# mLSTM tiles: waits by scan direction, the next tile's mask products and scores moved between this tile's products, and output tiles gated earlier

## The reference, cut to what matters

```python
dmat = jnp.where(mask, b[..., :, None] - b[..., None, :] + ic[..., None, :], -jnp.inf)
s = jnp.einsum('bhtd,bhsd->bhts', qc, kc) * jnp.exp(dmat - m_t[..., None])
num = w_inter[..., None] * jnp.einsum('bhtd,bhde->bhte', qc, cm) + jnp.einsum('bhts,bhse->bhte', s, vc)
den = w_inter * jnp.einsum('bhtd,bhd->bht', qc, nv) + s.sum(axis=-1)
h = num / jnp.maximum(jnp.abs(den), jnp.exp(-m_t))[..., None]
...
h = h_f + flip(h_b)
...
ha = rms_norm(ha.astype(xm.dtype), P['mlstm_norm_w'][j].reshape(A_HEADS, A_V_DIM)).reshape(bsz, n_tok, A_HEADS * A_V_DIM)
ha = ha * jax.nn.sigmoid(oa)
```

## Time and profile before

| | |
|---|---|
| median of 3 runs | 1601.32 us (1595.04 to 1603.25) |
| the profiled execution | 1601.95 us, span 1600.1 us, granted clock 0.918 |
| TensorE busy | 1356.6 us, 85% of the span |
| VectorE, ScalarE, GpSimd busy | 1002.8, 802.8, 428.6 us |

### The profile page before, as it was taken

How to read it: one execution, slowest core, us unless ns; L and a number is a source line. 1 busy time by engine, 2 the same in 40 slices (tenths; PEclk the granted TensorE clock), 3 DMA queues, 4 the chain that set the end, 5 groups by cost and what they waited for, 6 DMA issues and landing times. The chain is left out here.

```text
span 1600.1 us, 17702 instructions
## 1 busy us (share of the span) xinstructions
PE 1356.6 (85%) x6661; PEld 944.4 (59%) x6661; DVE 1002.8 (63%) x1331; ACT 802.8 (50%) x1135; POOL 428.6 (27%) x257
## 2 busy tenths in 40 slices
PE   3389998768779299999998999988779299999995
PEld 0366566744468166666666878654458266666663
DVE  0624623366564688888876625935554688888875
ACT  0421312354342277777775348554332277777772
POOL 0200203034400204433441021534400205433440
PEclk7699999689899599999998999999899599999997
DMA  9378860050051799999984012040051799999954
GB/s 358 145 285 340 310 227 16 1 197 1 1 212 66 279 341 367 385 378 379 379 307 118 1 57 57 5 197 1 1 203 74 272 344 366 384 381 383 380 183 163
DMA packets 64300, 341.73 MB, mean 214 GB/s; under 512 B 16796, under 2 KB 21512, under 8 KB 45784
## 3 DMA queue, kind: packets, MB, share of 16 engines
q1 hardware_dynamic: 58168, 319.96, 52.4%
q0 software_dynamic: 6048, 20.65, 5.5%
HBM read 316.67 MB, written 23.91 MB: 213 GB/s over the span
## 5 line engine op out<-in xcount | busy, mean ns | idle before, releaser
L1791 DVE TENSOR_TENSOR wlow<-wraw,proj_rounded 128x2048 fp32r<-128x2048 f32 x96 | 216.9, 2287 | 5.2 <-ACT proj_rounded L1733 5.2
L1641 POOL TENSOR_TENSOR modrow<-modrow,proj 80x1024 f32<-80x1024 f32 x30 | 133.2, 4439 | 309.2 <-ACT modrow L1759 309.2
L1670 PE MATMUL psum<-wlow,proj_rounded 128*80 128x512 f32 x512 | 202.4, 395 | 0.0
L1733 ACT ACTIVATE proj_rounded<-wraw 128x2048 fp32r<-128x2048 f32 x96 | 180.0, 1909 | 9.2 <-PEq L1322 9.2
L1669 PE MATMUL psum<-proj_rounded 128*80 128x512 f32 x376 | 151.3, 402 | 2.1 <-DVE proj_rounded L1796 2.1
L1671 PE MATMUL psum<-proj_rounded 128*80 128x512 f32 x376 | 148.6, 395 | 0.0
L1255 POOL TENSOR_SCALAR ring<-ring,small 128x640 f32<-128x640 f32 x64 | 100.0, 1566 | 167.4 <-DVE small L1202 166.6
L1228 ACT ACTIVATE ring<-psum,small 128x640 f32<-128x640 f32 (+1 forms) x80 | 56.7, 709 | 103.3 <-DVE small L1196 102.8
L1193 DVE TENSOR_REDUCE small<-psum 128x1 f32<-128x640 f32 (+1 forms) x80 | 57.2, 715 | 72.2 <-PE psum L1167 72.1
L1670 PE MATMUL psum<-wlow,small_rounded 128*80 128x512 f32 x256 | 100.8, 394 | 0.0
L1791 DVE TENSOR_TENSOR wlow<-wraw,xr_rounded 128x2048 fp32r<-128x2048 f32 x32 | 73.3, 2291 | 43.6 <-ACT xr_rounded L1733 43.6
(11 more groups left out here) (461 smaller groups left out, 3256.7 us busy)
## 6 DMA issues: line engine op xcount, KB each, us to landing
wraw<-in_exp_w_gate_dram SPq DMA_DIRECT2D x32, 2048.0 KB, 13.8
wraw<-in_exp_w_up_dram SPq DMA_DIRECT2D x32, 2048.0 KB, 12.6
wraw<-in_exp_w_down_dram SPq DMA_DIRECT2D x32, 2048.0 KB, 13.7
ring<-in_ada_w_dram SPq DMA_DIRECT2D x29, 1024.0 KB, 6.8
hold<-in_ada_w_dram SPq DMA_DIRECT2D x14, 1024.0 KB, 6.7
ring<-in_ev_w_in_dram SPq DMA_DIRECT2D x4, 2048.0 KB, 11.8
xr<-x_rows SPq DMA_DIRECT2D x15, 512.0 KB, 8.2
proj<-mod_rows SPq DMA_DIRECT2D x12, 512.0 KB, 5.5
```

The source lines that it names most:

```text
L1641: pool.tensor_tensor(ye[0:CAP, :], ye[0:CAP, :], g2[0:CAP, :], ALU.mult).then_inc(s["ye"], 1)
L1670: pe.matmul(dst, xs[:, 0, k, :], wl, start=False, stop=False)
L1733: act.activation(high_of(m, h), raw_of(m, h), ACT.Copy).then_inc(s["high"], 1)
L1791: dve.tensor_tensor(low_of(m, h), raw_of(m, h), high_of(m, h), ALU.subtract).then_inc(s["low"], 1)
```

## The change

- TensorE: mask products and scores of tile 0 come first. Then, within tile i, `bounds(i + 1, 0)` stands ahead of direction 0's products, and `bounds(i + 1, 1)` and `scores(i + 1)` stand between direction 0's and direction 1's. Direction 0's products wait for `fwd` only, direction 1's for `both`.
- ScalarE: `exponent(i + 1, 0)`, `forward(i)`, `exponent(i + 1, 1)`, `squares(i)`. `forward` waits for direction 0's divisors. Before the last `forward` it takes the square root for the first four tiles.
- VectorE: divisors by direction (`divisors(i, d)`), the rest of `normalise` as `backward(i)`, the next tile's weights between them. In the last tile the reciprocals of four tiles and the gating of the first one stand between the two directions' divisors, three more gatings after `backward`.
- `HA` lies in the columns of queries and keys (from `C_QA`); sums of squares and gatings go by the order of work.

```diff
--- before.py
+++ after.py
@@ -812,7 +812,7 @@
         def mlstm():
             s = {n: sem("ml_" + n) for n in ("kw", "upd", "carry", "qw", "qt", "qc", "ow",
                                              "mask", "E", "st", "W", "inter", "out", "own", "dn", "fwd", "both", "sq", "ssq", "root",
-                                             "ready", "turned", "copied", "h")}
+                                             "last_root", "ready", "turned", "copied", "h")}
             s2 = Carve(ringf)
             E = s2(2, 2, 4, P)
             CS = s2(2, ST - 1, 2, AV + 1)
@@ -823,7 +823,7 @@
             w = num_w
             dn = small[:, 0:8]
             ssq, rs = small[:, 32:52], small[:, 64:84]
-            HA = proj[:, :, C_VA:C_VA + AH * AV]
+            HA = proj[:, :, C_QA:C_QA + AH * AV]
             OA = proj[:, :, C_OA:C_OA + AH * AV]
 
             def turn_of(d, i):
@@ -914,30 +914,36 @@
                         mm.then_inc(s["out"], 1)
 
                     def turn(n):
+                        t = order[n]
                         pe.wait_ge(s["ready"], n + 1)
                         if n >= 4:
                             pe.wait_ge(s["copied"], n - 3)
                         for k in range(4):
-                            mm = pe.transpose(bank(n % 4)[:, k * P:(k + 1) * P], HA[:, n, k * P:(k + 1) * P], ident[:, :])
+                            mm = pe.transpose(bank(n % 4)[:, k * P:(k + 1) * P], HA[:, t, k * P:(k + 1) * P], ident[:, :])
                         mm.then_inc(s["turned"], 1)
 
                     for u in range(len(sums)):
                         add_sum(u)
                         turn_query(u)
                     pe.wait_ge(s["qc"], len(steps))
+                    bounds(0, 0)
+                    bounds(0, 1)
+                    scores(0)
                     for i, t in enumerate(order):
-                        bounds(i, 0)
-                        bounds(i, 1)
-                        scores(i)
+                        if i + 1 < TILES:
+                            bounds(i + 1, 0)
                         if i == 0:
                             pe.wait_ge(s["carry"], len(sums))
                         else:
                             pe.wait_ge(s["fwd"], i)
+                            from_state(i, 0)
+                        from_tile(i, 0)
+                        if i + 1 < TILES:
+                            bounds(i + 1, 1)
+                            scores(i + 1)
+                        if i:
                             pe.wait_ge(s["both"], i)
-                        for d in range(2):
-                            if t != PT:
-                                from_state(i, d)
-                        from_tile(i, 0)
+                            from_state(i, 1)
                         from_tile(i, 1)
                     for n in range(TILES):
                         turn(n)
@@ -955,7 +961,7 @@
                         ex.then_inc(s["E"], 1)
 
                     def forward(i):
-                        act.wait_ge(s["dn"], i + 1)
+                        act.wait_ge(s["dn"], 2 * i + 1)
                         for n in range(4):
                             r, j = n // 2, n % 2
                             h = 2 * j + r
@@ -972,20 +978,23 @@
                         t = turn_of(d, i)
                         act.wait_ge(s["qt"], n + 1)
                         act.activation(mq1[:, d, :, t * P:(t + 1) * P], bank(2 + n % 2, 256).rearrange("p (j c) -> p j c", j=2), ACT.Copy).then_inc(s["qc"], 1)
+                    exponent(0, 0)
+                    exponent(0, 1)
                     for i in range(TILES):
-                        exponent(i, 0)
-                        if i:
-                            forward(i - 1)
-                        exponent(i, 1)
-                        if i:
-                            squares(i - 1)
-                    forward(TILES - 1)
-                    squares(TILES - 1)
+                        if i + 1 < TILES:
+                            exponent(i + 1, 0)
+                        if i == TILES - 1:
+                            act.wait_ge(s["ssq"], i)
+                            act.activation(rs[:, 0:4 * i], ssq[:, 0:4 * i], ACT.Sqrt, scale=1.0 / AV, bias=EPS).then_inc(s["root"], 1)
+                        forward(i)
+                        if i + 1 < TILES:
+                            exponent(i + 1, 1)
+                        squares(i)
                     act.wait_ge(s["ssq"], TILES)
-                    act.activation(rs, ssq, ACT.Sqrt, scale=1.0 / AV, bias=EPS).then_inc(s["root"], 1)
-                    for n in range(TILES):
+                    act.activation(rs[:, 4 * TILES - 4:4 * TILES], ssq[:, 4 * TILES - 4:4 * TILES], ACT.Sqrt, scale=1.0 / AV, bias=EPS).then_inc(s["last_root"], 1)
+                    for n, t in enumerate(order):
                         act.wait_ge(s["turned"], n + 1)
-                        act.activation(xT[:, 4:8, n * P:(n + 1) * P], bank(n % 4).rearrange("p (k c) -> p k c", k=4), ACT.Copy).then_inc(s["copied"], 1)
+                        act.activation(xT[:, 4:8, t * P:(t + 1) * P], bank(n % 4).rearrange("p (k c) -> p k c", k=4), ACT.Copy).then_inc(s["copied"], 1)
 
                 @block.vector
                 def _(dve):
@@ -1020,20 +1029,22 @@
                         e4 = E[:, i % 2, d].rearrange("p (r j) n -> p r (j n)", r=2)
                         dve.tensor_tensor(e4, e4, psum[:, 0:2, 0:2 * P], ALU.mult).then_inc(s["W"], 1)
 
-                    def normalise(i):
+                    def divisors(i, d):
                         t = order[i]
-                        dve.wait_ge(s["out"], 2 * i + 2)
-                        if i:
+                        dve.wait_ge(s["out"], 2 * i + d + 1)
+                        if i and d == 0:
                             dve.wait_ge(s["fwd"], i)
-                        d8 = psum[:, 4:8, 0:258].rearrange("p b (j e) -> p b j e", e=129)[:, :, :, AV]
-                        d4 = d8.rearrange("p (d r) j -> p d r j", d=2)
-                        dn4 = dn.rearrange("p (d r j) -> p d r j", d=2, r=2)
-                        for d in range(2):
-                            neg = dve.scalar_tensor_tensor(out=dn4[:, d], in0=d4[:, d], scalar=-1.0, in1=col(2, d, t, 0, AH).rearrange("p (j r) -> p r j", r=2),
-                                                           op0=ALU.mult, op1=ALU.max)
-                        own.link(neg)
-                        own.link(dve.tensor_tensor(dn.rearrange("p (b j) -> p b j", j=2), dn.rearrange("p (b j) -> p b j", j=2), d8, ALU.max))
-                        dve.reciprocal(dn, dn).then_inc(s["dn"], 1)
+                        d4 = psum[:, 4 + 2 * d:6 + 2 * d, 0:258].rearrange("p r (j e) -> p r j e", e=129)[:, :, :, AV]
+                        own4 = dn[:, 4 * d:4 * d + 4]
+                        dn4 = own4.rearrange("p (r j) -> p r j", r=2)
+                        own.link(dve.scalar_tensor_tensor(out=dn4, in0=d4, scalar=-1.0, in1=col(2, d, t, 0, AH).rearrange("p (j r) -> p r j", r=2),
+                                                          op0=ALU.mult, op1=ALU.max))
+                        own.link(dve.tensor_tensor(dn4, dn4, d4, ALU.max))
+                        dve.reciprocal(own4, own4).then_inc(s["dn"], 1)
+
+                    def backward(i):
+                        t = order[i]
+                        dve.wait_ge(s["dn"], 2 * i + 2)
                         dve.wait_ge(s["fwd"], i + 1)
                         for n in range(4):
                             r, j = n // 2, n % 2
@@ -1044,9 +1055,8 @@
                         ins.then_inc(s["both"], 1)
 
                     def reduce(i):
-                        t = order[i]
                         dve.wait_ge(s["sq"], i + 1)
-                        dve.tensor_reduce(ssq[:, 4 * t:4 * t + 4], sq.rearrange("p (h d) -> p h d", d=AV), AX.X, ALU.add).then_inc(s["ssq"], 1)
+                        dve.tensor_reduce(ssq[:, 4 * i:4 * i + 4], sq.rearrange("p (h d) -> p h d", d=AV), AX.X, ALU.add).then_inc(s["ssq"], 1)
 
                     for u in range(4):
                         weigh_keys(u)
@@ -1054,22 +1064,37 @@
                         next_state(u)
                         if u + 4 < len(sums):
                             weigh_keys(u + 4)
-                    for i in range(TILES):
-                        weights(i, 0)
-                        weights(i, 1)
-                        if i:
-                            reduce(i - 1)
-                        normalise(i)
-                    reduce(TILES - 1)
-                    dve.wait_ge(s["root"], 1)
-                    own.link(dve.reciprocal(rs, rs))
-                    for t in range(TILES):
-                        dve.wait_ge(s["ow"], t + 1)
+                    def gated(n):
+                        t = order[n]
                         for h in range(AH):
                             sl = slice(h * AV, (h + 1) * AV)
```

(26 more changed lines are left out.)

## The result

The kernel after ran in 1576.80 us (median of 4 runs, 1575.80 to 1579.38), against 1600.41 us before (4 runs, 1595.04 to 1603.25): 0.9859 of the time, with a 95% interval of 0.9829 to 0.9888. Forecast were 1579.5, with 1572 to 1591. Two later series with the same kernel gave ratios of 0.9882 (0.9852 to 0.9912) and 0.9872 (0.9847 to 0.9898).

A forecast was written before the change was run, and what follows sets the result against it. No engine is full; a chain through several engines sets a 10.17 us period. The stage's last copy moves from 332.6 to 309.3, 23.3 us, less 1.3 for hand-overs: 22 us, 1601.32 to 1579.5, range 1572 to 1591.

The forecast's parts named there:

- The chain: Tile loop: waits through ScalarE, VectorE and TensorE set a period of 10.17 us, to become 4.76 with TensorE never waiting over 0.1.
- the allowance: 1.3 us taken off the 23.3 us gain for hand-overs that fit less closely, 0.3 in each of four periods.
- Prices at full clock: TensorE's work per tile, priced mostly from tile 0: bounds 0.63, scores 0.52, from_state 0.52, from_tile 0.97, together 4.76 us.
- Rival (b): Loop: clock stays at half, TensorE needs 8.8 us per tile, gain 12.8 us, time 1588.5; chance 0.16.
- the closing part: Stage's end after the last tile's backward: 9.2 us becomes 7.2, 2.1 less, ended by five ScalarE copies behind the last Sqrt.
- The two ideas of the loop: Releases by direction and next tile's work between the products, costed together: period 4.76 us in place of 10.17.
- Cost 0.3: Last tile: reciprocal and four gatings between the two directions' divisors bring VectorE to the second at 300.6, costing 0.3 us.
- the early root: Last tile: Sqrt for the first four tiles ahead of the last forward delays what stands behind it by 0.2 us.
- The table load: Sqrt table load on ScalarE takes 1.28 us, without the skill's added drain of about 1.38, which would make about 1.2 worse.
- (a): Loop: hand-overs slip 1.4 us per tile at full clock, gain 17.7 us, time 1583.6; chance 0.20.
- (c): Loop: a ring of waits between engines lets nothing overlap, period 16.7 us, time 1625, slower; chance 0.02.
- (d): Attention after the stage: starts 22 us earlier but at half clock for long, total about 1600; chance 0.05.

The follow-up runs named there:

- experiment 5: Kernel after without the mask's product ahead of each direction's row terms (causal mask left out): stage 35.14 us against 36.45, last three periods mean 4.73.
- experiment 6: Kernel after with ten VectorE copies ahead of the loop, for which TensorE waits: pause 8.69 us, stage 39.04 us from its first mask product against 36.45.
- experiment 2: Kernel after with TensorE waiting for both halves of the tile before ahead of direction 0's products: stage 40.34 us against 36.45, period 6.51, ratio to before 0.9905.
- experiment 7: Kernel after with 23 products that nobody reads between the closing part's transposes: stage 36.22 us against 36.45.
- experiment 9: Kernel after with gating shared with GpSimd and 18 filling products between the last transposes: stage 36.36 us, median 1573.50 us.
- experiment 1: Kernel before with seven unread products in TensorE's pause in each tile but the first: stage 46.82 us against 58.13, ratio 0.9938, median 1587.13 us.
- experiment 4: Kernel after with the old closing part (one square root over all tiles after the last, then all twenty gatings): stage 37.95 us against 36.45.
- experiment 3: Kernel after with each tile's masks, scores, exponents and weights back behind the previous tile's products: stage 37.30 us against 36.45, period 5.57, ratio to before 0.9888.
- experiment 8: Kernel after with GpSimd gating the first four tiles inside the loop, VectorE and ScalarE only scaling: stage 34.54 us against 36.45.

## Why the prediction was right, point by point

**The chain** of the kernel before, and that it would dissolve: right. The period was forecast at 4.76 us, or 5.06 with the allowance, and is 5.14. TensorE is the bound, as said; experiment 5 shows it. To the end of `backward` in the last tile the stage gained 19.6 us (48.90 and 29.28 from its start), where 21.1 less the 1.3 for hand-overs were forecast; behind it 2.06 (9.23 and 7.17), where 2.1 were.

**Prices at full clock.** The sum was nearly right by terms that were off both ways. `bounds` I took from two mask products at the head of the loop, 0.63; between other products it takes 0.81. `from_state`, taken as `scores`, 0.52, takes 0.65. `scores` takes 0.44 for 0.52 and `from_tile` 0.89 for 0.97. Net 2 x 0.18 + 2 x 0.13 - 0.08 - 2 x 0.08 = +0.38 in each period, where the allowance for hand-overs had 0.3. So the allowance was near the right size by luck, for another cause: no hand-over slips within the periods, TensorE's starts follow each other.

**The clock.** Rival (b) was given 0.16. The clock held at 1.00 through the loop in every run on the new order that began with it there, and came back in the one that didn't (experiment 6). The page of the Trainium skill (TensorE: Matmul & The Clock Gate, A second HAM failure mode) tells of a kernel in which short idles between groups make it fall again and again. Here idles of 1.3 us in each period of 6.5 (experiment 2) did not bring it down. Nor is a pause of over 2 us the mark, as rival (b) reads the rows: one of 2.47 left the clock up (experiment 7), and behind one of 1.85 it was down (experiment 9). The prediction had the clock's price in the new order, 10.5 us in rival (b), but not its share in the gain: in the old order it is 11.3 us (experiment 1). At full clock the two orders differ by 46.82 - 37.95 = 8.9, and the closing part has 1.5.

**The two ideas of the loop overlap.** The prediction costed them together. With the new closing part and full clock, the old order would stand at 46.82 - 1.50 = 45.3 (a sum of two runs, not one run). Interleaving alone brings 5.0 from there (40.34), single release alone 8.0 (37.30), both 8.9.

**The closing part** is where terms were mis-sized. Experiment 4 gives it 1.50 us: behind `backward` it brings 2.51, where the forecast had 2.1, and ahead of it the gating between the divisors and the early root cost 1.01, where the text has "Cost 0.3" and 0.2. The 0.3 compares the wrong two times of the prediction's placement, the second divisors' start (300.6) with `forward`'s end (300.3). Without the gating the second divisors run beside `forward`: in experiment 4 they start at 298.64, and `backward` then waits 0.68 us for ScalarE. By the prediction's own times `backward` would have ended there near 301.4, not 302.2, a cost of 0.8, or 1.0 with the root's 0.2. The sum was not hurt, since it goes by the 302.2. In the kernel after, `forward` starts 0.80 after the first divisors do and not 0.59 as in experiment 4, since it stands behind the early root. VectorE comes to the second divisors only at 303.34, 0.3 after `forward` has ended (301.87 + 1.13), and `backward` follows 0.6 behind them.

From `backward` on the forecast was 7.2, measured 7.17. That is luck in part, for the copies don't set it: VectorE's queue (three gatings, the sum, the last gating to 310.42) and then transposes at half clock (1.11) end it. What the old end took there, 9.2, is 9.68 behind the faster loop (experiment 4), where the last tile's transposes still run at the lower clock.

**The table load.** Sqrt starts at the end of the load here too (300.45 + 1.28, and 301.74), without the drain that the Trainium skill adds (ScalarE: Activation LUTs, What ACT_TABLE_LOAD costs). ScalarE's squares before the load end at 300.43, so no drain lies ahead of it either.

**Rivals (a), (c), (d).** No slip (a); the ring of waits in (c) never closes (experiment 3 takes it apart, and the stage is 0.85 longer); the attention takes 107.8, 109.05 and 108.9 us in the three traces of the kernel after and 109.25 before, so nothing is given back (d). Of 22.7 us less span (1600.1 and 1577.4), the stage gives 21.7; the rest is of the size by which unchanged parts differ between executions.

## What to carry to other kernels

Read the granted clock beside each chain: where TensorE paused for 2 us in each period here, the products on the chain ran at half speed, and keeping it busy in the pause, even with products that nobody reads, gave half of what the better order gave. Such products can also stand in the way of real ones, as at the end of experiment 9. Release each half of an accumulator as soon as its own reader is done; once that is done, further interleaving had 0.85 us left here. And price an instruction from where it stands between others, not from the head of a burst.

## What the runs showed of the hardware

The copies that held TensorE in experiment 6 were to take about 5 us in all and took 8.46. The line's own view:

```profile
L1078 DVE COPY ring<-ring x10: 426/428/1489, 275.0 to 283.0; 128x512 f32<-128x512 f32 x10
```

and the last six in VectorE's timeline:

```profile
280.69 2.73 DVE L1078 COPY ring<-ring 128x512 f32<-128x512 f32 x6
```

The columns of the first are the shortest, median and longest in ns. Six of them run in 2.73 us once GpSimd's last product ended, at 273.67 + 6.70 = 280.37. The first four took 5.7 us beside GpSimd's products, one of them 1.49. GpSimd's five took 6.70 in place of 6.18. The other VectorE instructions in that place didn't do so: the weights of tile 0, which read PSUM, take 0.69 beside the same products (kernel after, 278.28 and 279.31). This agrees with the Trainium skill (SBUF — State Buffer, SBUF: two separate sides), by which VectorE's copies between SBUF tiles and GpSimd take an exclusive pair of ports in turns. The scalings of experiment 8 had no GpSimd product beside them: the last one ended at 300.22, and the first scaling began at 300.90.
